# First quad of a two-block transformer kernel: products ordered by operand with a wait for each, nine warming matmuls fewer, and the last addition and squares in two column halves

## The reference, cut to what matters

```python
# first thing: norm of x and the projection of the first mixer (cut)
q, k, v, gate, qi, ki, wi = split_cols(rms_norm(x, a_norm) @ a_w_in, A_WIDTHS)
...
# last thing: down projection of the feed-forward layer, the residual sum, and the norm of the sum
x = x + (jax.nn.silu(h2 @ w_ffn_gate[l]) * (h2 @ w_ffn_up[l])) @ w_ffn_down[l]
return rms_norm_2(x, norm_f_w)
```

## Time and profile before

| | before |
|---|---|
| device time, median of 3 | 2247.11 us (2246.83 to 2247.27) |
| span of the profiled execution, first to last instruction | 2246.6 us |
| PE busy | 2226.5 us, 99% |
| DVE busy | 1388.1 us, 62% |
| ACT busy | 1181.6 us, 53% |
| HBM read | 396.06 MB, 177 GB/s over the span |

### The profile page before, as it was taken

How to read it: one execution, slowest core, us unless ns; L and a number is a source line. 1 busy time by engine, 2 the same in 40 slices (tenths; PEclk the granted TensorE clock), 3 DMA queues, 4 the chain that set the end, 5 groups by cost and what they waited for, 6 DMA issues and landing times.

```text
span 2246.6 us, 28822 instructions
## 1 busy us (share of the span) xinstructions
PE 2226.5 (99%) x11450; PEld 1838.2 (82%) x11450; DVE 1388.1 (62%) x1860; ACT 1181.6 (53%) x1637; POOL 115.1 (5%) x101
## 2 busy tenths in 40 slices
PE   9999999999999999999999999999999999999998
PEld 7888888888888887888788888888888888888886
DVE  5677765757765677675665556765555455554555
ACT  5546665646665654554454555555444344534443
POOL 0003210002220121000000000000000000000000
PEclk9999999999999999999999999999999999999999
DMA  7456676656686764445644456667666566656663
GB/s 259 145 169 182 189 212 224 206 169 190 191 243 204 215 188 133 150 132 169 206 150 150 150 169 214 212 220 227 196 214 197 191 205 203 206 189 201 191 206 131
DMA packets 311302, 426.77 MB, mean 190 GB/s; under 512 B 118976, under 2 KB 119136, under 8 KB 311040
## 3 DMA queue, kind: packets, MB, share of 16 engines
q1 hardware_dynamic: 309008, 417.82, 58.9%
q0 software_dynamic: 1584, 6.16, 1.0%
q10 hardware_dynamic: 576, 0.95, 0.1%
HBM read 396.06 MB, written 2.10 MB: 177 GB/s over the span
## 4 chain that ended last, share of the span: by engine, by line
PE 95%; DVE 2%; ACT 1%; DMA 1%; issue 1%; POOL 0%; DVEq 0%; ACTq 0%
PE ACC L1004 29%; PE ACC L1006 28%; PE ACC L1005 28%; ACT arena L1033 1%; DVE WL L2104 1%; PE SCPV L597 1%; DMA W<-in_a_w_in 0%; PE TP L544 0%; ACT WH L1033 0%; PE SCPV L741 0%; PE SCPV L596 0%; PE SCPV L735 0%; PE SCPV L556 0%; PE SCPV L636 0%; PE SCPV L604 0%
## 5 line engine op out<-in xcount | busy, mean ns | idle before, releaser
L2104 DVE TENSOR_TENSOR WL<-W,WH 128x1024 fp32r<-128x1024 f32 x740 | 911.0, 1236 | 536.5 <-PE ACC L1006 360.1
L1004 PE MATMUL ACC<-WH,XH 128*128 128x512 f32 x2592 | 1040.0, 401 | 3.7 <-ACT arena L1033 2.3
L1006 PE MATMUL ACC<-WH,XL 128*128 128x512 f32 x2592 | 1011.1, 390 | 0.0
L1005 PE MATMUL ACC<-WL,XH 128*128 128x512 f32 x2592 | 1009.4, 389 | 0.0
L1033 ACT ACTIVATE WH<-W 128x1024 fp32r<-128x1024 f32 x740 | 757.0, 1051 | 322.5 <-PE ACC L1006 227.4
L1004 PEld LDWEIGHTS ACC<-WH,XH 128*128 128x128 f32 x2592 | 487.0, 188 | 112.2 <-issue 5.4
L1006 PEld LDWEIGHTS ACC<-WH,XL 128*128 128x128 f32 x2592 | 486.5, 188 | 104.2
L1005 PEld LDWEIGHTS ACC<-WL,XH 128*128 128x128 f32 x2592 | 487.4, 188 | 95.6 <-issue 1.2
L1004 PE MATMUL ACC<-WH,HH 128*128 128x512 f32 x328 | 128.8, 393 | 0.0
L1006 PE MATMUL ACC<-WH,HL 128*128 128x512 f32 x328 | 127.7, 389 | 0.0
L1005 PE MATMUL ACC<-WL,HH 128*128 128x512 f32 x328 | 127.7, 389 | 0.0
(11 more groups left out here) (308 smaller groups left out, 1368.2 us busy)
## 6 DMA issues: line engine op xcount, KB each, us to landing
W<-in_w_in SPq DMA_DIRECT2D x84, 1024.0 KB, 5.0
W<-in_a_w_in SPq DMA_DIRECT2D x47, 1024.0 KB, 5.3
W<-in_w_ffn_gate SPq DMA_DIRECT2D x44, 1024.0 KB, 5.2
W<-in_w_ffn_up SPq DMA_DIRECT2D x44, 1024.0 KB, 5.3
W<-in_w_ffn_down SPq DMA_DIRECT2D x44, 1024.0 KB, 5.1
W<-in_b_w_in SPq DMA_DIRECT2D x40, 1024.0 KB, 5.2
W<-in_a_w_out SPq DMA_DIRECT2D x16, 1024.0 KB, 5.9
W<-in_b_w_out SPq DMA_DIRECT2D x16, 1024.0 KB, 6.2
```

What stands on the lines that cost most here:

```text
L1004: MM(out, hx, WH[:, k, 0:ch.width], start=q == 0 and k == 0, stop=False)
L1005: MM(out, hx, WL[:, k, 0:ch.width], start=False, stop=False)
L1006: ins = MM(out, lx, WH[:, k, 0:ch.width], start=False, stop=last and k == QK - 1)
L2104: TT(tiles_of(M.WL[K.pair(n)], ch, half), tiles_of(M.W[n % 3], ch, half), tiles_of(M.WH[n % 3], ch, half).bitcast(F32), ALU.subtract).then ...
```

## The change

There are four edits. The first quad of the first chunk is issued by a new function, `first_half`, once for each half: four products XH with WH (both t), a visit's side tasks, four XL with WH, four XH with WL, and again side tasks. Each of the three groups waits for its own operand alone. `WARM[1]` falls from 22 to 13. The last `take` adds in two column halves, each with an event of its own (`last_added`), and ACT squares in two halves, each into a column of its own of `M.ss`, which gets one column more.

```diff
-WARM = (10, 22)
+WARM = (10, 13)
...
-    M.ss, M.rs = sb("sums_of_squares", [P, 5, NC_D, TB]), sb("reciprocal_roots", [P, 5, TB])
+    M.ss, M.rs = sb("sums_of_squares", [P, 5, NC_D + 1, TB]), sb("reciprocal_roots", [P, 5, TB])
...
+    def first_half(ch, half):
+
+        nonlocal visit
+        hi, lo, WH, WL = M.hi[ch.xs], M.lo[ch.xs], M.WH[0], M.WL[K.pair(0)]
+        tiles = [(t, k, slice(t * P, (t + 1) * P)) for t in range(TB) for k in range(half * HK, (half + 1) * HK)]
+        pe.wait_ge(*at("turned_hi", ch.fresh, half))
+        pe.wait_ge(*at("weights_rounded", 0, half))
+        for t, k, ts in tiles:
+            MM(M.ACC[t][:, :], hi[:, k, ts], WH[:, k, :], start=k == 0, stop=False)
+        sides_of(tasks, K.starts, visit, live)
+        visit += 1
+        pe.wait_ge(*at("turned", ch.fresh, half))
+        for t, k, ts in tiles:
+            MM(M.ACC[t][:, :], lo[:, k, ts], WH[:, k, :], start=False, stop=False)
+        pe.wait_ge(*at("weights_rest", 0, half))
+        for t, k, ts in tiles:
+            ins = MM(M.ACC[t][:, :], hi[:, k, ts], WL[:, k, :], start=False, stop=False)
+            if k % HK == HK - 1:
+                ins.then_inc(*did("multiplied", 0, half, t))
+        sides_of(tasks, K.starts, visit, live)
+        visit += 1
...
+            if n == 0:
+                for half in range(QK // HK):
+                    first_half(ch, half)
+                continue
...
-        act.wait_ge(*at("acc_taken_dve", f"d.p2c{NC_D - 1}", t))
-        A(K.square_room[:, t, :], M.X[:, t, (NC_D - 1) * CH:], ACT.Square, accum_out=M.ss[:, 4, NC_D - 1, t:t + 1]).then_inc(*did("last_squares", t))
+        for part in range(2):
+            act.wait_ge(*at("last_added", t, part))
+            cs = slice((NC_D - 1) * CH + part * CH // 2, (NC_D - 1) * CH + (part + 1) * CH // 2)
+            ins = A(K.square_room[:, t, part * CH // 2:(part + 1) * CH // 2], M.X[:, t, cs], ACT.Square, accum_out=M.ss[:, 4, NC_D - 1 + part, t:t + 1])
+        ins.then_inc(*did("last_squares", t))
...
+            if ch is K.chunks[-1]:
+                for part in range(2):
+                    cs = slice(part * CH // 2, (part + 1) * CH // 2)
+                    TT(x[:, cs], acc[:, cs], x[:, cs], ALU.add).then_inc(*did("last_added", t, part))
+                return
```

More of the change, by code:

```diff
@@ L1558, in roots @@
         sums, room = M.root_of["norm"], M.root_room["norm"]
-        V.tensor_reduce(sums, M.ss[:, i].rearrange("p c t -> p t c"), AX.X, ALU.add).then_inc(*did("square_totals", l))
+        V.tensor_reduce(sums, M.ss[:, i, 0:NC_D].rearrange("p c t -> p t c"), AX.X, ALU.add).then_inc(*did("square_totals", l))
         dve.wait_ge(*at("square_totals", l))
```

## The result

| | before | after |
|---|---|---|
| device time, median of 8 | 2247.56 us (2246.83 to 2248.26) | 2253.51 us (2253.10 to 2256.19) |
| ratio, 95% interval | | 1.0027 [1.0018, 1.0036] |
| profiled execution | span 2246.6 us | 2253.58 us, span 2252.3 us |

The account below looks back on a forecast made before the run. PE was taken as the bound, busy 99% of 2246.6 us; head 0 and tail -0.04 gave a span of 2246.56, plus 0.5 to the median, 2247.07, say 2247.1 us. Own range 2246.6 to 2247.7; 8-in-10 range 2246.0 to 2247.9.

Parts of the forecast that it names:

- From 36.11 on: After PE's pause at the start of the second chunk: everything stays at its old time within 0.1 us.
- a low clock: Rival: PE's 1.92 us pause at 34.19 lets TensorE's clock fall; +1.8 us, 2248.9 us; chance 0.06.
- The term of the head: First 36 us: first product 1.27 us sooner, 0.92 left at quad 1, all waited away before ACT's reading of ACC; 0.
- The term of the tail: After the last product, t = 1: addition and squares in halves end sooner; -0.04 us, bounds -0.15 and +0.10.
- the head's gain: Rival: the head's gain reaches the end, ACT's reading of ACC moving with PE; -0.92 or -1.27 us; chance 0.10.
- The warming: Rival: too little warming, first products at the low level; at most 1.6 us, taken by slack, 2247.1; no separate chance.
- Quad 3's load: Rival: in the head, it lands over 0.3 us later; up to +0.7, 2247.8 us; chance 0.06, as much sooner 0.03.

Follow-up runs that it names:

- e1: The kernel before with only the tile of the sums of squares one column wider, the column read by nobody; 2253.56 us, ratio 1.0027.
- e2: The changed kernel with the old tile size, the last norm's five sums in a small tile allocated last, all others at old places; 2247.32 us, ratio 0.9999.
- e3: The kernel before with 64 unused bytes a partition ahead of HH, moving only HH, HL and the tiles behind them; 2253.42 us, ratio 1.0026.
- e9: The kernel before with ACT's squares of x for the first norm moved from visits 8 to 11 to visits 4, 5, 8 and 9; 2245.63 us, ratio 0.9993.
- e10: The changed kernel with every tile in its old place, plus ACT's first-norm squares moved to visits 4, 5, 8 and 9; 2245.58 us, ratio 0.9992.
- e7: The kernel before with 64 unused bytes ahead of x, the first tile, so everything moves and all distances stay; 2247.54 us, ratio 1.0001.
- e5: The kernel before with 64 unused bytes ahead of WH0, moving WH, WL and all behind, HH and HL too; XH and XL stay; 2261.73 us, ratio 1.0061.
- e11: The kernel before with 448 unused bytes ahead of HH, 64 short of a multiple of 512; 2248.55 us, ratio 1.0007.
- e6: The kernel before with 64 unused bytes between HH and HL, so HH stays and HL moves; 2251.61 us, ratio 1.0015.

## Why the prediction was wrong, point by point

- **The step that failed** is this sentence: "The wider `M.ss` and the sum over five values in place of four I cost at nothing: it is one 128x1 instruction in both, and the other norms still read four." It costs the tile by the instructions that touch it. What it does is to move every tile behind it by 64 bytes, HH and HL among them, and their 1056 products then take 5.8 ns longer each: +6.1 us. Shown by e1 (this edit alone, +6.3), e2 (all but this, +0.1) and e3 (HH's place alone, +6.2).
- "From 36.11 on, all instructions and waits are the old ones" was true, and yet nothing followed from it: "Everything from there on at its old time" did not. That the same instructions take the same time was a tacit step. It held for the products with XH and XL (228.0 ns in both) and not for those with HH and HL.
- The range was too narrow for the same reason. All of its bounds came from the first 36 and the last 9 us; no term was there for the 2200 us between, in which 5.8 ns on one product in eight made 6 us. It gave a loss of more than 0.2% a chance of 0.02, and tied it to a low clock alone.
- The term of the head, 0, was right, and by its own mechanism: first product and quad 1 sooner, group 2 of x met at 14.2, a pause of 1.86 for 1.92, the reading of ACC at 35.37 for 35.30. e2 measures the sum of head and tail: 2247.32 beside 2247.26 of before. e9, on the kernel before, took away the late reading and the pause went with it.
- The term of the tail had the right sign and half the size: -0.04 forecast, -0.08 in the traces, inside its bounds. That this shows in the time can't be told. The rule of the Trainium skill, "VectorE: DVE Perf Modes", section "The TRN2 errata", which asks for tiles of at least 512 elements since each instruction pays a fixed latency, would by itself have made the tail longer. The trace agrees for one engine (0.42 and 0.40 us for the half squares, 0.63 for the whole), but the two engines overlap, and the tail got shorter.
- The rivals: the head's gain didn't reach the end (the pause of 1.86 us took it, and e10 shows that it hardly does even with the squares early). The clock didn't fall in a pause of 1.86 us. The warming was enough: the first four products take 1.17 us, the four from 13.03 take 1.18. Transposes alone had raised the rate, ten of the identity and eight of x: the 13 behind them take 1.58 us, 0.12 apiece as the 22 in 2.57 before, and the first ten 2.40, 0.24 apiece. That is against the rule of the Trainium skill, "TensorE: Matmul & The Clock Gate", section "Part 4: PE-mode transpose", by which transposes don't raise the clock. Quad 3's load was not late: ACT's WH on it starts at 23.00, before at 22.93, in an execution whose identity landed 0.18 later. The true case was none of them: a slower side whose mechanism was not on the list.

## What to carry to other kernels

An edit to the size of a tile is an edit to the address of every tile allocated behind it; before costing it at nothing, list which matmul operands move, and by how much against the operands that they meet. Here new tiles belong at the end of the allocation, or padded so that the distance from stationary to moving operand stays a multiple of 256 bytes: that was worth 6 us of 2247, six times the pause of 1.00 us on which the forecast turned. And where PE waits for another engine further on, a gain ahead of that wait is only slack; the wait must go first (e9), and then the next one in its chain shows (e10).

## What the runs showed of the hardware that was not expected

- The rate of a stream of 128x512 matmuls, fp32r, each with its own weight load, depends on the distance in bytes between its stationary and its moving operand in a partition of SBUF: 228.2 ns a product at a multiple of 256, 233.9 at +64, 233.0 at +128, 230.0 at -64. The absolute place makes no difference (e7, 228.1, and e5). Neither the granted clock (1.00) nor the record of the weight load shows it; the matmul's record does: 393 ns growing to 397 for WH with HH, 389 to 395 for WH with HL.
- The price has a sign: +64 costs three times what -64 costs (5.8 ns; 1.8 in e11, 2.0 in e5). And a product isn't slowed by its own pair alone (e6). One could guess at a conflict between two readings of the same memory, the weights of the next product and the columns of this one. It isn't shown: no run here looks inside, and in e6 the step in which the moved weights were loaded grew by 2.5 ns, and the one behind it by 8.5. Distances that aren't a multiple of 64 were not tried.
